# One core of Trainium2: when the second expert's weights are asked for, and the order of the work at the end of the mixing stage

## What is computed

```python
h = _rms_norm(x, norm1_w[i])
u = jnp.einsum('btd,dc->btc', h, w_in[i])
y_a = _rwkv7_mixer(u_r, ...)
y_b = _hgrn2_mixer(u, lb_all[:, i], hgrn_gnorm_w[i])
x = x + jnp.einsum('btc,cd->btd', jnp.concatenate([y_a, y_b], axis=-1), w_out[i])
h2 = _rms_norm(x, norm2_w[i]).reshape(B * T, D)
x = x + _hier_moe(h2, ...).reshape(B, T, D)
...
return _rms_norm(x, final_norm_w)
```

## Time and profile before

| | us |
|---|---|
| median of 3 runs | 2351.63 (2350.96 to 2352.99) |
| the profiled execution, its own time | 2347.96 |
| span of its profile | 2346.1 |
| TensorE busy | 2228.4 (95%) |
| VectorE, ScalarE, GpSimd busy | 1032.1, 713.7, 407.5 |

### The profile page before, as it was taken

The page is one execution under the profiler, slowest core; times in us unless marked ns, Lnnn a source line. Parts: engine busy times, 40 slices in busy tenths (PEclk is TensorE's granted clock), DMA queues, the critical chain, the costliest instruction groups (busy, mean ns, idle before and its releaser), DMA issues. The chain is left out here.

```text
span 2346.1 us, 64499 instructions
## 1 busy us (share of the span) xinstructions
PE 2228.4 (95%) x28004; PEld 1463.3 (62%) x28004; DVE 1032.1 (44%) x2219; ACT 713.7 (30%) x1441; POOL 407.5 (17%) x506
## 2 busy tenths in 40 slices
PE   7999999999999999999998989998799999999996
PEld 4444444445555555555557756656688888888884
DVE  3336776834644744644655766644111111111114
ACT  4124454623544544544542322221000000000003
POOL 1012222310000000000002210102533333333321
PEclk9999999999999999999997999997899999999998
DMA  4103344443343333333338843454799999999997
GB/s 142 36 23 126 135 157 139 171 106 92 92 111 83 99 97 93 93 96 91 88 108 243 260 147 117 158 180 146 252 362 353 331 355 334 361 352 334 362 330 290
DMA packets 359966, 436.66 MB, mean 186 GB/s; under 512 B 164994, under 2 KB 296198, under 8 KB 351536
## 3 DMA queue, kind: packets, MB, share of 16 engines
q1 hardware_dynamic: 343232, 397.94, 50.0%
q0 software_dynamic: 14384, 35.19, 6.1%
q10 hardware_dynamic: 2112, 0.01, 0.1%
HBM read 329.84 MB, written 104.50 MB: 185 GB/s over the span
## 5 line engine op out<-in xcount | busy, mean ns | idle before, releaser
L1198 PE MATMUL h_pp<-hT,r_wcol 128*128 128x512 f32 x832 | 413.0, 619 | 3.3 <-ACT h_iraw L1313 3.3
L2858 PE MATMUL e_ps_gu<-e_xT,e_wg 128*128 128x128 f32 x2048 | 236.4, 277 | 12.6 <-DVE e_xT L2971 12.6
L2858 PEld LDWEIGHTS e_ps_gu<-e_xT,e_wu 128*128 128x128 f32 x2048 | 233.6, 192 | 14.3 <-issue 14.3
L2858 PEld LDWEIGHTS e_ps_gu<-e_xT,e_wg 128*128 128x128 f32 x2048 | 233.5, 194 | 13.2 <-DVE e_xT L2971 12.8
L2858 PE MATMUL e_ps_gu<-e_xT,e_wu 128*128 128x128 f32 x2048 | 233.8, 275 | 0.0
L2867 PE MATMUL e_ps_y<-e_wd,e_hid 128*128 128x512 f32 x512 | 225.1, 592 | 0.7 <-DVE e_hid L3030 0.7
L1198 PEld LDWEIGHTS h_pp<-hT,r_wcol 128*128 128x128 f32 x832 | 141.5, 189 | 124.0 <-issue 108.8
L522 PE MATMUL h_pp<-hT,r_wcol 128*128 128x512 f32 x480 | 215.2, 607 | 1.3 <-DVE hT L794 1.3
L2983 DVE TENSOR_SCALAR e_y<-e_ps_y,e_row 128x512 f32<-128x512 f32 x31 | 23.3, 751 | 337.7 <-PE e_ps_y L2867 337.6
L522 PEld LDWEIGHTS h_pp<-hT,r_wcol 128*128 128x128 f32 x480 | 92.6, 195 | 113.7 <-issue 112.0
L2867 PEld LDWEIGHTS e_ps_y<-e_wd,e_hid 128*128 128x128 f32 x512 | 94.8, 190 | 108.7 <-issue 107.1
(11 more groups left out here) (419 smaller groups left out, 3406.7 us busy)
## 6 DMA issues: line engine op xcount, KB each, us to landing
e_wg<-in_moe_w_gate_dram SPq DMA_DIRECT2D x32, 2048.0 KB, 12.6
e_wu<-in_moe_w_up_dram SPq DMA_DIRECT2D x32, 2048.0 KB, 12.8
e_wd<-in_moe_w_down_dram SPq DMA_DIRECT2D x32, 2048.0 KB, 12.7
r_wcol<-in_w_in_dram SPq DMA_DIRECT2D x35, 512.0 KB, 5.5
ar<-r_ar SPq DMA_DIRECT2D x24, 512.0 KB, 2.7
kb<-r_kb SPq DMA_DIRECT2D x24, 512.0 KB, 2.8
m_ar<-ar SPq DMA_DIRECT2D x48, 256.0 KB, 4.7
m_kb<-kb SPq DMA_DIRECT2D x48, 256.0 KB, 3.5
```

Source lines behind the costliest of these rows:

```text
L1198: last = nc.tensor.matmul(pp[n % 2][:], wcol[(k + 2) % 3][:, c], self.hT[:, c, span(s)], start=c == 0, stop=c == KT - 1)
L2858: last = nc.tensor.matmul(ps[:, q * P:(q + 1) * P], w[u][:, c, q * P:(q + 1) * P], xT[u][:, c * P:(c + 1) * P], start=c == 0, stop=c == KT ...
```

## The change

It has three parts.

1. SyncE's wait ahead of the second expert's up and down weights has one more condition: `x_loaded[1]` at 64, which is all four gathers of the second block's rows landed.
2. The last tile (n = 11, `LAST`) is normed in another way. VectorE multiplies each half of x1 by the norm's weight as soon as the half is there; TensorE transposes that, and the factor 1/rms is applied by VectorE to the 36 logits, in the instruction that adds the bias, and by ScalarE to the tile that is stored as h2. The squares are summed by half, and the second half of `turn` uses the bank `o_ps_k`, which the scan has left, for this tile and all that are turned after the scan. `routed` waits for each half of the transposed tile apart.
3. The list's tail, from n = 11 on, is written out by hand (`endings`), in another order.

```diff
-                for n in range(-2, TILES + 3):
+                for n in range(-2, TILES - 1):
...
-                return out
+                return out + endings()
+
+            def endings():
+
+                e, g = TILES - 1, LAST_PAIR - 1
+                return [(name, args, cost, e) for name, args, cost in (
+                    ("turn", (e - 2, 0), 1.1), ("rank", (g - 1,), 0.4), ("half", (e, 0, 0), 3.5), ("place", (g - 1,), 0),
+                    ("msq", (e - 1,), 0), ("m_root", (e - 1,), 0), ("turn", (e - 2, 1), 1.1), ("routed", (e - 2,), 1.7),
+                    ("h2n", (e - 1,), 0), ("half", (e, 1, 0), 3.5), ("choose", (g, 0), 0), ("turn", (e - 1, 0), 1.1),
+                    ("choose", (g, 1), 0), ("turn", (e - 1, 1), 1.1), ("half", (e, 0, 1), 3.5), ("routed", (e - 1,), 1.7),
+                    ("x1_half", (e, 0), 0), ("choose", (g, 2), 0), ("weigh", (g,), 0), ("half", (e, 1, 1), 3.5),
+                    ("x1_half", (e, 1), 0), ("x1", (e,), 0), ("msq", (e,), 0), ("rank", (g,), 0.4), ("turn", (e, 0), 1.1),
+                    ("turn", (e, 1), 1.1), ("m_root", (e,), 0), ("place", (g,), 0), ("h2n", (e,), 0), ("routed", (e,), 1.7))]
...
+            turn_bank = lambda n, h: bank_k if ("turn", n, h) in bank_k.use else bank_x
+            turn_ps = lambda n, h: ps_k[:].rearrange("p j n -> p (j n)") if turn_bank(n, h) is bank_k else ps_x[:]
...
+                     turn=lambda n, h: (bank_k if h and scan_over else bank_x).claim(("turn", n, h)),
...
-                    self.waits(sp, dve_t.at("h2", n))
+                    self.waits(sp, act_last.at("h2", 0) if n == LAST else dve_t.at("h2", n))
...
                 def turn(n, h):
-                    self.waits(eng, dve_t.at("h2", n), bank_x.free(("turn", n, h)))
+                    self.waits(eng, dve_last.at("high" if h else "low", 0) if n == LAST else dve_t.at("h2", n),
+                               turn_bank(n, h).free(("turn", n, h)))
...
                 def routed(n):
-                    self.waits(eng, bank_x.done(("turn", n, 1)), bank_y.free(("logits", n)), (params, 16 * 5))
+                    self.waits(eng, bank_y.free(("logits", n)), (params, 16 * 5))
                     for c in range(KT):
+                        if c % PAIRS == 0:
+                            self.waits(eng, turn_bank(n, c // PAIRS).done(("turn", n, c // PAIRS)))
...
+                def x1_half(n, h):
+                    if n == LAST:
+                        self.waits(eng, dve_x.at("x1" if h else "low", n), dve_var.at("sumsq", UNITS - 1))
+                        nc.scalar.activation(by_k(sq[h][:]), hgrn(FINISHED[n]) if h else rwkv(n), ACT.Square,
+                                             accum_out=ss[:, n + h:n + h + 1]
+                                             ).then_inc(*(act_t.inc("sq") if h else act_last.inc("sq")))
...
+                def routed(n):
+                    if n == LAST:
+                        self.waits(eng, dve_t.at("inv", n))
+                        nc.scalar.activation(work[n % RING_X][:], work[n % RING_X][:], ACT.Copy, scale=rq[:, n:n + 1]
+                                             ).then_inc(*act_last.inc("h2"))
...
+                    if n == LAST:
+                        half = slice(h * SPAN, (h + 1) * SPAN)
+                        self.waits(eng, dve_x.at("x1" if h else "low", n))
+                        nc.vector.tensor_tensor(by_k(work[u][:, half]), hgrn(t) if h else rwkv(n), by_k(n2w[:, half]), ALU.mult
+                                                ).then_inc(*dve_last.inc("high" if h else "low"))
...
+                        nc.vector.tensor_tensor(ss[:, n:n + 1], ss[:, n:n + 1], ss[:, n + 1:n + 2], ALU.add
+                                                ).then_inc(*dve_last.inc("sum"))
...
+                    if n == LAST:
+                        self.waits(eng, dve_t.at("inv", n))
+                        nc.vector.scalar_tensor_tensor(self.logits[:, FINISHED[n]], ps_y[:, 0:NG + NE], rq[:, n:n + 1], rbias[:],
+                                                       ALU.mult, ALU.add).then_inc(bank_y.read, 1)
+                        return
...
-                self.waits(sp, (self.e_first_row, 16))
+                self.waits(sp, (self.e_first_row, 16), (x_loaded[1], 64))
```

34 lines of the change are left out of this document (23 added, 11 removed).

## The result

| | before | changed |
|---|---|---|
| median of four runs each, us | 2351.3 | 2331.33 |
| lowest to highest, us | 2346.73 to 2352.99 | 2328.36 to 2334.35 |
| profiled execution, its span, us | 2347.96, 2346.1 | 2331.13, 2329.6 |

The ratio is 0.9918, with a 95% interval from 0.9899 to 0.9937. The prediction was 2332.0 us.

What follows compares the result with a forecast made beforehand. TensorE was taken as the bound, busy 2228.4 of 2346.1 us, with gains only from its waits and slow-clock matmuls. Gains of 5.0, 12.6 and 2.0 us, 19.6 together, took the 2351.63 median to 2332.0, range 2328.0 to 2341.0.

Steps and rivals of the forecast that it cites:

- Part 1: Common stage's end: new order and late scale bring the last tile's logits 5.0 us earlier, bounds 4.1 and 5.4.
- The table load, with or without a drain: ScalarE's last root: load costs 1.28 us without drain; the skill's 1.38 us drain would make the sum 0.8 smaller.
- The h2 store and the last `weigh`: Behind the last logits: both later, but costed at nothing; a microsecond or two if the store had to be waited for.
- Part 2: Ahead of block 1: weights requested behind the rows remove all 12.60 us of TensorE's idle time, with 2.2 us to spare.
- Part 3: Block 1's gate matmuls: without idle time ahead they take 7.31 us instead of 9.31, a gain of 2.0 us.
- Block 2's weights: Block 2's gate matrix lands 2.2 to 3.9 us before TensorE wants it, costed at nothing; rival that it waits, chance 0.16.
- The sum: Whole kernel: 5.0 + 12.6 + 2.0 = 19.6 us gained, giving a median of 2332.0 us.
- The slower rival: Expert stage: GpSimd's scatter-adds set the pace if landings average 1.1 us longer; near 2356 us at 1.9; chance 0.03.

Runs made afterwards that it cites:

- e3: The change, but the second expert's up weights (one 2 MB transfer) are asked for as soon as the first row is there; ratio 0.9922 to the kernel before.
- e2: The change without SyncE's added wait for the second block's rows; ratio 0.9980 to the kernel before.
- e0: The changed kernel run once more, unaltered; ratio 0.9912 to the kernel before.
- e10: The change with five added copies on GpSimd ahead of each block's scatter-add; ratio 1.0216 to the kernel before.
- e11: The change with 32 unused matmuls of `ident` by `ident` in TensorE's gaps ahead of block 0; ratio 0.9909 to the kernel before.
- e7: The change with 30 unused matmuls of `ident` by `ident` in TensorE's gaps ahead of block 0; ratio 0.9901 to the kernel before.

## Why the prediction was right, point by point

- **Part 1, gain 5.0.** Measured 5.7 at the logits and 5.8 at block 0, above the upper bound of 5.4. The last projection ends 18.7 us behind its start, 19.1 were predicted: the stall of 0.5 us at tile 9's logits did not happen. x1 is whole at 19.7 (predicted 20.0). The logits' matmuls ran at full clock, where I had taken a value between the two levels; the predicted time for full clock was 24.2, measured 23.9. The choice of the middle was the mis-sized term, by 0.4; the stall that did not happen is most of the other 0.3. What held the logits back at full clock was ScalarE's root (until 1610.74) as much as VectorE's `place` (until 1610.71).
- **The table load, with or without a drain.** ScalarE's load starts at 1609.25 and takes 1.28, and the root starts at 1610.54, 0.01 behind its end. The 1.38 us of drain that the Trainium skill (ScalarE: Activation LUTs, What ACT_TABLE_LOAD costs) adds do not show here either. The trace's reading was the right one.
- **The h2 store and the last `weigh` cost nothing**, as costed: no wait in block 0's or block 1's chain names them, and behind the logits everything keeps its old distance. From the logits to the issue of the last `slots` piece it is 13.7 us, as before.
- **Part 2, 12.6.** All of the idle time is gone, with 2.5 us to spare (predicted 2.2), for the reason given: each of the three landings is at the length of its quiet row. The Trainium skill (DMA: Bandwidth & Descriptors, Queues, rings and completion order) has each DMA engine switch between its queues packet by packet. e3 agrees in part: from 1630 on the small transfer's packets pass beside the load's. But none passed in the 3 us before, and the landing took 6.6 us instead of 2.1; what held them there no run shows. The prediction's use of the rule, that a deeper backlog does not lengthen a small transfer once there is one at all, holds for `slots`: 6.6 us behind 2 MB in e3, 6.9 before and 7.2 in e2, both behind 4.5 MB.
- **Part 3, 2.0.** 7.31 instead of 9.31, as said. Not foreseen was that block 0's own gate matmuls vary with where in them the clock comes back: 7.41 to 8.99 over the fourteen profiles. That alone moves the sum by up to 1.5 us from profile to profile.
- **Block 2's weights cost nothing**, but the margin was 1.5 us, not 2.2 to 3.9. The step from the first request to the landing was short: 24.2 us passed, where I had 21.6, or 23.3 with half a megabyte of gathers. Two blocks' gathers run in this stretch, not one's. The DMA views from the first request to the landing (before 1626.88 to 1648.5, the change 1637.74 to 1661.9) have GpSimd's queue with 0.28 and 1.07 MB:

```profile
q0 software_dynamic: 254, 0.28, 6.1%
```

```profile
q0 software_dynamic: 547, 1.07, 14.0%
```

All queues together moved 7.69 MB at 356 GB/s before and 8.84 MB at 366 GB/s in the change.
- **The sum.** 19.6 predicted behind the common start, 19.6 measured. That they agree so closely is partly luck. Part 1's surplus of 0.7 is still there at block 3, where the gain is 20.3, and is lost again at the end of the kernel; from the second profile of the kernel before to e0 the gain is 21.0 (763.0 to 742.0). The same goes for 2332.0 against 2331.33, a median of runs that lie 6 us apart.
- **The slower rival** did not come true by its own condition: it needed landings 1.1 us longer on average, and GpSimd's waits for them grew by 0.5 us per block (312.5 to 328.6 over 30). The 32.4 us of waits for results vanished at no cost; GpSimd enters the loop later against TensorE. The form of its price, the lag per block beyond the spare times 30 blocks, is what e10 bears out (2.4 us times 27 rounds are 65 of 69 us). The spare came to 1.4 us there, 3.8 of added work less 2.4 of lag, against the 1.1 of the prediction.

## What to carry to other kernels

Before a big prefetch is issued, look at which small dependent transfers are still ahead of the first use, and put the request behind the last of them if its own deadline allows; work out both deadlines, since here the two spares are 2.5 and 1.5 us. A reordering may pay only together with a shorter chain: the new order lost 1 us by itself and made 6 with the scale moved behind the matmuls (the shorter chain alone was not run). When a helper engine has no spare time left, its lag can stay hidden behind the buffers for many blocks. It is still owed if the end of the kernel waits for the helper's last result, so price it as lag per block times all blocks, with nothing taken off for the buffers.

## What the runs showed of the hardware

- A small DMA of GpSimd's, issued 0.9 us behind one 2 MB weight load, landed 6.6 us after its issue instead of 2.1, and the next small one behind it was not held up (e3). Its packets began to move only 3 us after the issue and then passed side by side with the load's. With three loads of 4.5 MB in all asked for within 1 us and a fourth behind them, three small ones in a row were held up.
- TensorE's granted clock fell from 1.00 to 0.50 near 1602 in e11 with the engine recorded as busy without a gap since 1597.4 (mostly matmuls of 128x36 and 128x1), and near 1610 in e7 with no gap since 1606.4. It came back during unbroken work in both, also with matmuls whose result nobody reads (e11: busy without a gap from 1605.9, clock 0.50 until 1612 and 0.90 in 1612 to 1614).
- VectorE's last copy of block 0's transposes started 1.7 to 1.8 us behind the recorded end of these where many added matmuls stood ahead of them (e7, e11), against 0.04 in the change. The ends of matmuls are modelled in the records; whether the transposes really ended later was not tried.
- The same instructions ahead of the change took up to 12 us more or less from one profile to another (1576.9 to 1589.3 at the last projection). A shift of a few us ahead of an edit is no finding unless it repeats.
